# Values of a spatial branch with 512-wide operands, two of their tiles inside the last attention head, and modulation sums written out

## What is computed

```python
mod_x = einsum('bd,lde->lbe', silu(c), w_ada) + b_ada        # six vectors of 1024
hx = modulate(rmsnorm(x), sh1x, sc1x)                         # uses the first two of them
z = einsum('bnd,de->bne', hx, w_in)                           # q k v o g u vb ga gb
# four heads: a bidirectional mLSTM of q, k, v and gates, times sigmoid(o)  -> y_a
u = gelu(u_raw)
vb = rmsnorm(gelu(vb_raw), vnorm_g)                           # 'the values', 1024 x 1024
sv = einsum('gts,bcsgd->bctgd', w_sp, vb) + b_sp              # within chunks of 128 tokens
y_b = u * sv
merged = sigmoid(ga)*(y_a @ w_pa) + sigmoid(gb)*(y_b @ w_pb)
x = x + g1x * (merged @ w_out)
x = x + g2x * swiglu(modulate(rmsnorm(x), sh2x, sc2x))        # uses the other four
out = rmsnorm(x)
```

## Time and profile before

| | |
|---|---|
| median of 3 runs | 1909.56 us |
| the profiled execution | 1913.69 us, its span 1912.0 us |
| PE busy | 1833.0 us (96%) |
| DVE busy | 993.7 us (52%) |
| ACT busy | 553.3 us (29%) |
| POOL busy | 131.8 us (7%) |
| L1818, the 256-wide matmuls of `tokens` (heads and values) | 3 x 145 us, 283 ns each |
| L1803, the 512-wide matmuls of `channels` on `R_hi`, `whi` | 149.8 us, 393 ns each |

### The profile page before, as it was taken

How to read it: one execution, slowest core, us unless ns; L and a number is a source line. 1 busy time by engine, 2 the same in 40 slices (tenths; PEclk the granted TensorE clock), 3 DMA queues, 4 the chain that set the end, 5 groups by cost and what they waited for, 6 DMA issues and landing times.

```text
span 1912.0 us, 24057 instructions
## 1 busy us (share of the span) xinstructions
PE 1833.0 (96%) x9052; PEld 1534.2 (80%) x9052; DVE 993.7 (52%) x1571; ACT 553.3 (29%) x842; POOL 131.8 (7%) x131
## 2 busy tenths in 40 slices
PE   6898999999989999999999999999999999999987
PEld 3596797978879988888888878788888888788876
DVE  3676636556355543211221164675655566666657
ACT  5533132322312322111221131443334333311111
POOL 1001010100112000000100000000000000231200
PEclk9899999999999899999999999999999999999989
DMA  7200100202048201111411152122222232632302
GB/s 295 60 17 17 56 23 23 66 22 66 12 137 282 88 22 44 57 53 44 124 52 44 44 176 88 66 66 67 93 82 88 66 100 76 232 130 89 122 8 88
DMA packets 91337, 157.15 MB, mean 82 GB/s; under 512 B 4466, under 2 KB 73218, under 8 KB 86930
## 3 DMA queue, kind: packets, MB, share of 16 engines
q1 hardware_dynamic: 83906, 130.11, 20.3%
q0 software_dynamic: 7376, 26.28, 4.1%
HBM read 132.26 MB, written 24.12 MB: 82 GB/s over the span
## 4 chain that ended last, share of the span: by engine, by line
PE 89%; DVE 7%; issue 2%; ACT 1%; DMA 0%; DVEq 0%; SPq 0%; ACTq 0%
PE PD L1803 26%; PE PD L1818 11%; PE PD L2164 10%; PE PM L2164 10%; PE PD L2183 6%; PE PM L2183 6%; PE PD L2090 5%; PE PM L1803 5%; PE PM L2108 1%; PE PD L2108 1%; PE PM L2038 1%; PE PD L1885 1%; DVE Cst L1382 1%; PE PM L1844 1%; PE PM L1876 1%
## 5 line engine op out<-in xcount | busy, mean ns | idle before, releaser
L1803 PE MATMUL PD<-R_hi,whi 128*128 128x512 f32 x480 | 149.8, 393 | 1.7 <-DVE Hh L1405 1.7
L1803 PE MATMUL PD<-R_lo,whi 128*128 128x512 f32 x480 | 148.5, 391 | 0.0
L1803 PE MATMUL PD<-R_hi,wlo 128*128 128x512 f32 x480 | 148.1, 390 | 0.0
L1818 PE MATMUL PD<-whi,R_hi 128*128 128x256 f32 x512 | 145.0, 283 | 0.0
L1818 PE MATMUL PD<-wlo,R_hi 128*128 128x256 f32 x512 | 144.9, 283 | 0.0
L1818 PE MATMUL PD<-whi,R_lo 128*128 128x256 f32 x512 | 144.9, 283 | 0.0
L1158 DVE TENSOR_TENSOR wlo<-raw,whi 128x1024 fp32r<-128x1024 f32 x76 | 89.9, 1219 | 93.7 <-ACT whi L745 93.7
L745 ACT ACTIVATE whi<-raw 128x1024 fp32r<-128x1024 f32 x76 | 76.4, 1049 | 158.9 <-PE PD L1803 95.5
L1803 PEld LDWEIGHTS PD<-R_hi,whi 128*128 128x128 f32 x480 | 89.2, 188 | 21.4 <-issue 3.0
L1803 PEld LDWEIGHTS PD<-R_hi,wlo 128*128 128x128 f32 x480 | 90.4, 188 | 19.2
L1803 PEld LDWEIGHTS PD<-R_lo,whi 128*128 128x128 f32 x480 | 90.4, 188 | 19.1
(11 more groups left out here) (406 smaller groups left out, 4097.7 us busy)
## 6 DMA issues: line engine op xcount, KB each, us to landing
raw<-in_w_in SPq DMA_DIRECT2D x46, 512.0 KB, 4.5
rawF<-in_w_ff SPq DMA_DIRECT2D x44, 512.0 KB, 5.0
ada<-in_w_ada POOLq DMA_DIRECT2D x32, 512.0 KB, 5.9
f_dram<-Fo SPq DMA_DIRECT2D x11, 1024.0 KB, 4.8
w_raw<-in_w_ff SPq DMA_DIRECT2D x11, 1024.0 KB, 5.0
f_raw<-f_dram SPq DMA_DIRECT2D x11, 1024.0 KB, 6.9
ada_raw<-in_w_ada SPq DMA_DIRECT2D x8, 1024.0 KB, 19.8
raw<-in_w_in SPq DMA_DIRECT2D x20, 256.0 KB, 3.6
```

Of the source, the lines that this page charges most:

```text
L1803: i = mm(dst[:, e * HALF:e * HALF + width], wk[:, k, :], part, start=(k == 0 and step == 0), stop=(k == KT - 1 and step == 2))
L1818: i = mm(PD[s][:, e * HALF:e * HALF + CW], src[:, k, at], wk[:, k, :], start=(k == 0 and step == 0), stop=(k == KT - 1 and step == 2))
```

## The change

The values' tiles become 512 columns wide. `v_tile(i, t)` makes tile t (128 tokens) of half i (512 of the 1024 columns) with 8 x 3 matmuls whose moving operand spans two pieces at once: `N_V` and `N_V+1` in A and B for the first half, `N_V+2` and `N_V+3` in `wo_hi2`/`wo_lo2` for the second. Four PSUM banks take turns. Tiles (0,0) and (0,1) are issued inside the last head, ahead of the transposes of `Hh`; the other fourteen after it. ACT waits for the spill of the last head before its first Gelu, works tile by tile, and makes the next high parts before its tiles 2 and 5. DVE's loop over quarters is written out, and a quarter's split moves from behind its eight sums to behind its fourth sum. The buffers `wsp` and `bspB` are placed elsewhere in SBUF.

```diff
--- before.py
+++ after.py
@@ -235,14 +235,15 @@
...
                     uT = [sb(f"uT{k}", [P, NLAT], stack=s6) for k in range(2)]
-                    wsp = sb("wsp", [P, 4, P], stack=s6)
                     wsp_hi = sb("wsp_hi", [P, 4, P], F32R, s6)
                     wsp_lo = sb("wsp_lo", [P, 4, P], F32R, s6)
-                    bspB = sb("bspB", [P, 4, P], stack=s6)
                 with ExitStack() as s9:
                     wo_hi2 = sb("wo_hi2", [P, 2, 8 * CW], F32R, s9)
                     wo_lo2 = sb("wo_lo2", [P, 2, 8 * CW], F32R, s9)
                 Mb = sb("Mb", [P, KT, NLAT], stack=sU)
+                with ExitStack() as s10:
+                    wsp = sb("wsp", [P, 4, P], stack=s10)
+                    bspB = sb("bspB", [P, 4, P], stack=s10)
                 sg = sb("sg", [P, NLAT], stack=sU)
@@ -913,14 +914,14 @@
 
 
             act.wait_ge(pm_free, 10)
-            with act.Fori(0, 2) as i:
-                for cc in range(2):
-                    for p in range(4):
-                        act.wait_ge(tile_done, i * 8 + (T_V + 4 * cc + p + 1))
-                        nc.scalar.activation(V[:, 2 * p:2 * p + 2, ds(i * (2 * CW) + cc * CW, CW)],
-                                             PD[p % 2][:, :].rearrange("p (t n) -> p t n", t=2)[:, :, 0:CW],
-                                             ACT.Gelu_apprx_tanh).then_inc(slot_free[p % 2], 1)
-                    split_next(i * 2 + (N_V + 2 + cc), cc, i * 8 + (T_V + 4 * cc + 4))
+            act.wait_ge(spill, 16 * HEADS + 1)
+            for i in range(2):
+                for t in range(LT):
+                    if t in (2, 5):
+                        split_next(2 * i + t // 3 + (N_V + 2), 2 * (1 - i) + t // 3, T_V + LT if i else None)
+                    act.wait_ge(tile_done, i * LT + (T_V + t + 1))
+                    nc.scalar.activation(V[:, t, i * HALF:(i + 1) * HALF], held[0][t % 4], ACT.Gelu_apprx_tanh)\
+                        .then_inc(slot_free[t % 4 // 2], 1)
...
@@ -1437,21 +1438,19 @@
                 own.leave(HEADS)
-            with dve.Fori(0, 2) as i:
-                for cc in range(2):
-
-                    q = i * 2 + cc
-                    acc = Tacc[:, ds(q, 1), :]
-                    for k in range(KT):
-                        dve.wait_ge(pool_in[k % 4], q * 32 + (k // 4 * 16 + 16))
-                        src = ada2[k % 4][:, :].unsqueeze(1)
-                        if k == 0:
-                            v.tensor_scalar(acc, src, csil[:, 0, 0:1], None, ALU.mult).then_inc(ada2_used, 1)
-                        else:
-                            dve.wait_ge(ada2_used, q * KT + (k + 4))
-                            v.scalar_tensor_tensor(out=acc, in0=src, scalar=csil[:, 0, k:k + 1], in1=acc,
-                                                   op0=ALU.mult, op1=ALU.add).then_inc(ada2_used, 1)
-                    split_lo(i * 2 + (N_V + 2 + cc), cc)
+            for q in range(4):
+                acc = Tacc[:, q:q + 1, :]
+                for k in range(KT):
+                    dve.wait_ge(pool_in[k % 4], q * 32 + (k // 4 * 16 + 16))
+                    src = ada2[k % 4][:, :].unsqueeze(1)
+                    if k == 0:
+                        v.tensor_scalar(acc, src, csil[:, 0, 0:1], None, ALU.mult).then_inc(ada2_used, 1)
+                    else:
+                        dve.wait_ge(ada2_used, q * KT + (k + 4))
+                        v.scalar_tensor_tensor(out=acc, in0=src, scalar=csil[:, 0, k:k + 1], in1=acc,
+                                               op0=ALU.mult, op1=ALU.add).then_inc(ada2_used, 1)
+                    if k == 3:
+                        split_lo(q + (N_V + 2), (q + 2) % 4)
...
@@ -1897,6 +1896,20 @@
+            def v_tile(i, t):
+
+                pe.wait_ge(slot_free[t % 4 // 2], T_V // 2 + max(4 * i + t // 4 * 2 + t % 2, 1))
+                w = [q[:, :, :].rearrange("p b (k n) -> p k b n", k=KT) for q in ((whi2, wlo2), (wo_hi2, wo_lo2))[i]]
+                dst = held[0][t % 4].rearrange("p (b n) -> p b n", b=2)
+                for k in range(KT):
+                    if t == 0 and k % 4 == 0:
+                        for b in range(2):
+                            ready(N_V + 2 * i + b, k // 4)
+                    for step, (src, wk) in enumerate(((R_hi, w[0]), (R_hi, w[1]), (R_lo, w[0]))):
+                        last = mm(dst, src[:, k, t * P:(t + 1) * P], wk[:, k, :, :],
+                                  start=(k == 0 and step == 0), stop=(k == KT - 1 and step == 2))
+                last.then_inc(tile_done, 1)
+
             def head(h, first=False, last=False):
...
@@ -1981,11 +1994,14 @@
+                pe.wait_ge(h_written, h * 16 + 14)
                 if not last:
-                    pe.wait_ge(h_written, h * 16 + 14)
                     for m in range(2):
                         free(10 + m)
                         channels(m, n + 3, A, m, R_hi, R_lo)
+                else:
+                    v_tile(0, 0)
+                    v_tile(0, 1)
                 pe.wait_ge(hn_ready, h + 1)
...
@@ -2002,11 +2018,10 @@
-            with pe.Fori(0, 2) as i:
-                for cc in range(2):
-                    for p in range(4):
-                        pe.wait_ge(slot_free[p % 2], i * 4 + (T_V // 2 + 2 * cc + p // 2 + 1))
-                        tokens(p % 2, i * 2 + (N_V + cc), cc, R_hi, R_lo, (2 * p, 2 * p + 1))
+            for i in range(2):
+                for t in range(LT):
+                    if i == 1 or t >= 2:
+                        v_tile(i, t)
             pe.wait_ge(ada2_used, 4 * KT + 4)
```

## The result

The changed kernel takes 1916.33 us (median of 11 runs, 1913.08 to 1919.25), against 1909.56 for the one before beside it (11 runs, 1906.77 to 1914.03): ratio 1.0033, 95% interval 1.0024 to 1.0042. The medians are 6.8 us apart; by the ratio, which is taken over all runs, it is 6.3. The forecast was 1914.6. The profiled execution took 1918.65 us, its span is 1917.0.

A forecast was written before the change was run, and what follows sets the result against it. PE was taken as the bound. An earlier V end (-4.1 us), a middle hole (+7.6) and its low clock (+1.55) summed to +5.0 us: 1918.7 us profiled, 1914.6 us as median, range 1905.4 to 1918.6 us.

The forecast's parts named there:

- A: Forecast case: PE stands at a hole in the middle of V, +2.1 to +9 us, at 1914.6 us; chance 0.55.
- D: Rival: loads of 7.2 us and more make DVE's sums end last, column sums wait, +6 to +9 us; chance 0.11.
- the hole in the middle: PE between V's halves: waits from 594.2 to 601.8 us for the fourth weight's low-part split on DVE, 7.6 us.
- low clock: PE behind each hole: some 3.1 us at 1.2 GHz, costing 1.55 us per start.
- The wide operand: V matmuls on PE: 384 of 512 columns take 87.0 us against 92.15, saving 5.1 us.
- Tiles wait for piece B: Last head: the first tile waits for buffer B's low part, starts at 547.5 not 538.1; hole grows by 1.1 us.
- Shift of `sgo`, spill, loads and sums: Behind the transposes of `Hh`: everything waiting on DVE's `sgo` products moves 12.0 us later.
- Column sums at 646.9: End of V: column sums start at 646.9 us against 641.8, with DVE's 32 sums done at 641.9.
- B: Rival: weights come in time, PE never stands in the middle of V, -4.1 us, 1905.5 us; chance 0.10.
- C: Rival: near-shortest landings and steady clock, middle hole of some 4 us, 0 to +2 us; chance 0.20.
- E: Rival: the two tiles do fill the first hole in the last head, -4.3 us, 1905.3 us; chance 0.02.
- F: Rival: wide matmuls far closer spaced than in `out_tile`, but column sums wait for DVE, no change, 1909.8 us; chance 0.02.

The follow-up runs named there:

- E6: Changed kernel with 38 and 28 unused 512-column filler matmuls on PE ahead of tiles (0,0) and (1,0): 1911.07 us, ratio 1.0005.
- E3: Changed kernel with buffer B's low part split early in the last head, the third weight's before the sums, the fourth's behind the sixth sum: 1900.53 us, ratio 0.9943.
- E5: Changed kernel with each quarter's split moved from behind its fourth sum to behind its eighth: 1921.12 us, ratio 1.0066.
- E7: Changed kernel with buffer B's low part split early and the `ada` loads issued once the last numerators are done: 1898.63 us, ratio 0.9938.
- E4: Changed kernel with tiles (0,0) and (0,1) moved out of the last head, all 16 behind the transposes: 1903.53 us, ratio 0.9963.
- E1: Changed kernel with buffer B's low part split between the last numerator scalings of the last head: 1906.05 us, ratio 0.9976.
- E2: Changed kernel with the third weight's low part split before the sums, the fourth's behind the first quarter's sixth sum: 1912.33 us, ratio 1.0009.
- E8: Changed kernel with only the `ada` loads issued once the last numerators are done, not behind the spill: 1907.78 us, ratio 0.9981.

## Why the prediction was right

**What the number says, and what it doesn't.** The profiled execution was forecast at 1918.7 us and took 1918.65. That this is so close is luck: the column sums start 1.64 us later than forecast, and what lies behind them took 1.7 us less than in the kernel before. The medians differ by 6.8 us where 5.0 were forecast. And 1916.33 lies in A's own range (1911.8 to 1918) as well as in D's (1916 to 1919). It is the rows that tell the two apart: the hole in the middle is there, and the sums end 6.8 us before PE wants them.

**The sum of a stretch.** The parts add up: from the last numerator to the first row behind it, tiles, transposes, middle hole, low clock (by E6's pieces against the kernel's own), wait of the sums. For after 10.1 + 87.05 + 1.7 + 6.9 + 5.1 = 110.9 (measured 111.10); for E3 2.3 + 0.2 (a second short wait for piece B) + 87.05 + 1.8 + 3.0 = 94.3 (94.89); for E5 10.1 + 87.05 + 1.8 + 13.1 + 5.3 = 117.4 (117.53); for E7 2.3 + 0.2 + 87.05 + 1.8 + 1.4 = 92.7 (93.40). No further cause of more than 0.7 us is needed.

**Step by step.**
- The wide operand, -5.1 us: shown by E4, 87.08 against 92.15.
- Tiles wait for piece B, first at 547.5: measured 547.55, shown by E1.
- Shift of `sgo`, spill, loads and sums by 12.0 us: 13.1 for `sgo`, 13.75 for the first sum. The transposes came at 561.05, a good microsecond later than the sum made them (560), and that is the clock, below.
- First half packed to 594.2, the fourth weight's split at 600.5, a hole of 7.6 us: its last row starts at 595.25, the split at 601.22, the hole is 6.94. The hole is smaller though its end is later, since the low clock in the first half eats into it, which I had seen as possible for ACT's wait but not for the clock. Its cause is shown three ways: E2 moves the split, E5 moves it the other way, E8 moves the loads and with them the sums ahead of the split.
- ACT's new wait, costed at nothing: PE has no wait for a bank there.
- Column sums at 646.9 with DVE long done: 648.54, DVE done at 641.7 (642 by the sum).

**The mis-sized term** is the low clock. I priced each start behind a hole at 1.55 us, from 3.1 us at the low level behind the old one, where transposes ran first. The kernel after, stretches behind its two starts (547.55 and 602.58), PEclk third from the end:

```profile
547.00:552.00 5.00, 4.45 (x11) 3.51 (x12) 1.54 (x2) 0.00 (x0) 0.00 (x0) 0.50 0.01 3
552.00:553.00 1.00, 1.00 (x4) 0.81 (x3) 0.00 (x0) 0.00 (x0) 0.00 (x0) 0.56 0.00 0
...
602.00:605.00 3.00, 2.42 (x6) 1.97 (x7) 2.90 (x4) 0.00 (x0) 0.47 (x1) 0.50 0.94 306
605.00:608.00 3.00, 3.00 (x10) 2.32 (x9) 2.44 (x2) 0.00 (x0) 1.06 (x2) 0.59 0.99 334
608.00:610.00 2.00, 2.00 (x10) 1.61 (x9) 1.29 (x1) 0.00 (x0) 0.59 (x2) 1.00 1.10 389
```

0.56 in the microsecond from 552 is 0.88 us at the half level, so the low level ends at 552.9, 5.3 us behind the first start; in the same way 0.59 x 3 ends at 607.5, 4.9 us behind the second. Half of it is lost each time, 2.6 and 2.4 us; E6 gives back 2.5 and 2.5. Of the 1.64 us by which the column sums are later than forecast, 0.8 is the end of the hole (602.58 for 601.8: behind it stands the first low stretch) and 0.9 is the second low stretch.

The prediction also took the second hole that it drew on, at 1119 us, for three microseconds at 0.5. Its row says 0.59 over three, and the low level goes on in the row behind it in the kernel before:

```profile
1122.00:1125.00 3.00, 3.00 (x13) 2.39 (x12) 0.59 (x2) 0.00 (x0) 0.00 (x0) 0.84 1.02 379
```

Together that is 2.5 + 1.0 = 3.4 us at the low level, all of it in 512-wide tiles. Priced by it a start would have cost 1.7 us, which is still short of the 2.5 measured.

**The rivals.** B (weights in time) would show no hole; it is 6.9 us. C fell with it. D: the sums ended 6.8 us early; it holds only once the middle hole is gone and the loads still wait for the spill, by 1.9 us in E2 and 3.0 in E3. E is refuted by the start at 547.55. F by the spacing in E4.

The low clock alone doesn't make the slowdown: with both holes filled by idle work (E6) the kernel is at 1.0005, still short of E4's 0.9963, for PE is held for some 9 and 6 us all the same.

## What to carry to other kernels

A filler in a hole works only if its operands are there when the hole begins: look at what its widest instruction needs, and where the last of that stands in the order of the engine that makes it. What is put ahead of a hand-over moves all that hangs on it (here spill, loads, sums and a split 50 us further on) by the filler's length plus the wait that was not covered, and the second wait can be as large as the first. Price the start behind a hole with a range and not with one row: here I took 1.55 us and 2.5 were lost, and the low level held anything from 2.9 to 5.5 us from the first row behind a hole.

## What the runs showed of the hardware that I had not expected

In these traces the low clock lasted longer behind a hole when 512-wide tiles came first than when transposes did. From the first row behind the hole, the low level held 3.1 us before, where transposes ran first, and 5.3 and 4.9 us after; in E1's middle, with tiles, 4.1. E4, with the transposes first again (start at 542.27), and E1's middle (start at 587.89), by stretches:

```profile
542.00:545.00 3.00, 2.73 (x13) 2.76 (x14) 2.40 (x3) 0.00 (x0) 0.00 (x0) 0.50 0.02 5
545.00:546.00 1.00, 1.00 (x8) 0.91 (x7) 0.27 (x1) 0.00 (x0) 0.00 (x0) 0.92 0.00 0
```

```profile
588.00:592.00 4.00, 4.00 (x10) 3.13 (x11) 3.79 (x4) 0.00 (x0) 0.53 (x1) 0.50 0.88 274
592.00:593.00 1.00, 1.00 (x6) 0.82 (x5) 0.85 (x1) 0.00 (x0) 0.53 (x1) 1.00 0.98 347
```

In E4 0.92 in the fourth microsecond leaves 2.9 us at the low level; E1's is at 1.00 from 592. Worked out in the same way, the other starts with 512-wide tiles are 4.5 us (E2), 5.3 and 5.5 (E5) and 5.2 (E8). The one at 1119.19 in the kernel before speaks less clearly: PEclk was still 1.00 when the tiles came, after a hole of 4.33 us, and the low level ended 3.8 us behind the first row. So two starts with transposes gave 2.9 and 3.1 us, eight with wide tiles 3.8 to 5.5, each in one execution. No run puts both kinds of work behind the same hole, so whether the kind of work decides, or the length of the hole, or chance, stays open.

A wait of PE under 2 us (E3's 1.7 at tile 0, E7's 1.4 in the middle) left the clock at 1.00, while those of 6.5 us and more, and the one of 4.33 us before, were all followed by 1.2 GHz; E8 has one of each, 9.5 us with and 0.5 us without. The waits ahead of the column sums tell nothing here: the clock falls during these sums in the kernel before too, at 645.1, with no wait ahead of them.

A raw half of 512 KB took 3.7 us alone, and 13.2 us in E7 and E8. There it is issued in the middle of other transfers: in E7 at 557.7, the spill at 556.1, four `ada` loads between 557.0 and 561.2. In the kernel before, the same two halves were issued from 553.4 on, the first `ada` load at 558.7, and they took 5.6 and 6.5 us. The late half moved the critical wait from the sums to the weight. E7's last 1.4 us may be a matter of which queue's loads go first; it wasn't tried.
